# A routed-expert layer on one core: expert rows taken back to their tokens by TensorE and summed in SBUF, and the inputs of most experts fetched by indirect DMA

## The reference

```
x = x + concat(conv_out, pool_out) @ w_out
glog = hf @ w_rg + b_rg                    # hf = rmsnorm(x)
top_v, top_i = top_k(elog of the chosen group, 2)
w_top = softmax(top_v) * p_g
for e in range(32):
    a = silu(hf @ w_gate[e]) * (hf @ w_up[e])        # 2048 -> 512
    y = y + gates[:, e:e+1] * (a @ w_down[e])        # 512 -> 2048
x = x + y
y_prompt, y_sample = rmsnorm(x, g_final)
```

## Time and profile before

| what | value |
|---|---|
| median of 3 runs | 1323.94 us (1323.87 to 1324.67) |
| the profiled execution's own time | 1325.73 us |
| its span, first to last instruction | 1323.9 us |
| what lies around the span | 1.8 us |
| mean granted TensorE clock | 0.985 of full speed |
| TensorE busy, of the span | 94% |
| VectorE, ScalarE, GpSimd busy | 26%, 9%, 10% |
| HBM read, written | 457.20 MB, 20.80 MB |

### The profile page before, as it was taken

How to read it: one execution, slowest core, us unless ns; L and a number is a source line. 1 busy time by engine, 2 the same in 40 slices (tenths; PEclk the granted TensorE clock), 3 DMA queues, 4 the chain that set the end, 5 groups by cost and what they waited for, 6 DMA issues and landing times.

```text
span 1323.9 us, 15403 instructions
## 1 busy us (share of the span) xinstructions
PE 1240.6 (94%) x6286; PEld 686.6 (52%) x6286; DVE 350.8 (26%) x715; ACT 119.9 (9%) x242; POOL 134.1 (10%) x183
## 2 busy tenths in 40 slices
PE   9999999999999999988999999999999989989974
PEld 7777777777755445434443444434444544434421
DVE  5699974001342111120101011020101111010206
ACT  3100014000310000000000000000000000000022
POOL 6111394000000100000000000000000000000000
PEclk9999999999999999999999999999999999999998
DMA  9344424664579999999999999999999999999997
GB/s 289 136 151 149 142 96 147 248 254 159 210 281 416 409 429 426 427 430 430 427 430 431 430 430 425 429 429 428 430 429 433 428 430 427 428 428 427 424 422 264
DMA packets 77807, 465.26 MB, mean 351 GB/s; under 512 B 7263, under 2 KB 49375, under 8 KB 52243
## 3 DMA queue, kind: packets, MB, share of 16 engines
q1 hardware_dynamic: 71808, 455.36, 83.9%
q0 software_dynamic: 5392, 7.87, 2.0%
q10 hardware_dynamic: 571, 1.53, 0.3%
HBM read 457.20 MB, written 20.80 MB: 361 GB/s over the span
## 4 chain that ended last, share of the span: by engine, by line
PE 55%; DMA 42%; DVE 1%; ACT 0%; issue 0%; DVEq 0%; POOL 0%; SPq 0%; POOLq 0%
DMA arena<-in_w_up_dram 30%; PE bank L839 21%; PE bank L648 21%; DMA arena<-in_w_gate_dram 10%; PE bank L831 4%; PE bank L915 4%; DMA arena<-expert_rows 1%; PE bank L612 1%; PE bank L727 1%; DMA arena<-in_w_out_dram 1%; PE bank L596 1%; PE bank L745 0%; DVE arena L1464 0%; DVE arena L1476 0%; PE bank L581 0%
## 5 line engine op out<-in xcount | busy, mean ns | idle before, releaser
L839 PE MATMUL bank<-arena,xT 128*64 128x512 f32 x2040 | 456.5, 606 | 44.7 <-DMA arena<-in_w_up_dram 35.8
L839 PEld LDWEIGHTS bank<-arena,xT 128*64 128x64 f32 x2040 | 149.7, 140 | 348.9 <-issue 287.8
L648 PE MATMUL bank<-arena 128*128 128x288 f32 x1152 | 283.9, 408 | 0.0
L648 PEld LDWEIGHTS bank<-arena 128*128 128x128 f32 x1152 | 219.1, 191 | 63.5 <-issue 3.2
L915 PE MATMUL bank<-arena,aT 128*64 128x512 f32 x1024 | 228.7, 599 | 17.8 <-ACT aT L1129 15.2
L831 PEld LDWEIGHTS bank<-x1w,x1r 128*128 128x128 f32 x1536 | 173.9, 192 | 26.3 <-issue 25.2
L831 PE MATMUL bank<-x1w,x1r 128*128 128x128 f32 x1536 | 180.0, 277 | 0.9 <-ACT x1r L1094 0.9
L915 PEld LDWEIGHTS bank<-arena,aT 128*64 128x64 f32 x1024 | 72.5, 137 | 153.5 <-issue 138.7
L1495 DVE TENSOR_TENSOR a_sb<-sl_sb,bank 128x256 f32<-128x256 f32 x32 | 19.5, 608 | 476.0 <-ACT sl_sb L1127 476.0
L1658 POOL DMA_INDIRECT expert_rows<-ysb,cur_d x31 | 30.2, 973 | 836.7 <-DVE ysb L1515 809.9
L1240 DVE SCALAR_TENSOR_TENSOR arena<-arena,wdw 128x256 f32<-128x256 f32 x240 | 104.4, 514 | 0.1
(11 more groups left out here) (283 smaller groups left out, 446.5 us busy)
## 6 DMA issues: line engine op xcount, KB each, us to landing
arena<-in_w_down_dram SPq DMA_DIRECT2D x27, 4096.0 KB, 29.9
arena<-in_w_up_dram SPq DMA_DIRECT2D x41, 2048.0 KB, 20.7
arena<-in_w_gate_dram SPq DMA_DIRECT2D x19, 4096.0 KB, 26.7
arena<-in_w_gate_dram SPq DMA_DIRECT2D x16, 2048.0 KB, 20.5
arena<-in_w_up_dram SPq DMA_DIRECT2D x7, 4096.0 KB, 26.9
arena<-in_w_in_dram SPq DMA_DIRECT2D x11, 2048.0 KB, 8.1
arena<-in_w_gate_dram SPq DMA_DIRECT2D x19, 1024.0 KB, 9.7
arena<-in_w_out_dram SPq DMA_DIRECT2D x8, 2048.0 KB, 8.6
```

Source lines behind the costliest of these rows:

```text
L648: last = pe.matmul(ps[bank][:, 0:NTOK], wsl[a][:, k, cc * P:(cc + 1) * P], rhs[:, k, :], start=(n == 0), stop=(n == KT - 1))
L839: mm = pe.matmul(ps[4 + s][BLK * h:BLK * (h + 1), :], xgT[:, k, BLK * s:BLK * (s + 1)], w[:, :, 256 * h:256 * (h + 1)], start=(k == 0), st ...
```

## The change

The scatter of expert outputs, its DRAM tensor and the read back at the end are gone. In their place:

- `yrows` (the same SBUF as `ysb`) keeps a pair's 128 output rows whole, unscaled: two copies of 64 partitions by ScalarE and two by VectorE for each expert.
- For each pair VectorE makes `weighted_hot`, the one-hot table with the gate weights in it (six operations of 128x128, an add and a key update); TensorE transposes it in three pieces behind the second expert's gate and up, and VectorE copies the 288 columns to `to_token`.
- `combine_pair(i - 1)` runs behind gate and up of the first expert of pair i: four matmuls of 32 columns for the sample rows into bank 5 and eight of 128 columns by 512 for the prompt, into banks 2 and 3 in turn. VectorE adds each result to the token rows (`x1q`, and `acc_rows`, which lies in `x1r`), nine adds a pair. The third and later prompt matmuls wait for the add that frees their bank; down waits for all nine.
- ScalarE puts the residual rows in order in `acc_rows` during pair 0 (two copies of 128x2048, which stood before the last expert), and VectorE waits for them before pair 1.
- SyncE writes the 288 token rows to a DRAM tensor (2.36 MB) once the row copies are done, ahead of the first parts of expert 1. For pairs 2 to 15 GpSimd fetches 128 rows of 8 KiB by index, dropping empty slots, as soon as the fetch's buffer is free, which is when the inputs of the pair before are made.
- For those pairs `turn` takes the place of `select`: 16 matmuls in place of 48, with one scaled identity (`turn_table`) in place of `one_hot`.
- At the end all of pair 15 is combined on TensorE into eight banks, and added, squared and scaled in parts of 512 columns.
- The final gain's load waits for down of expert 30.

The core of the diff:

```diff
@@ sync, before the loop
             up_part(1, 1, 2, 8, ring_in[3])
+            sp.wait_ge(row_evac, 4 * TT)
+            for t in range(TT):
+                sp.dma_start(x1_dram[T0[t]:T0[t] + TS[t], :], x1r[0:TS[t], t, :]).then_inc(x1_out, 16)
             sp.wait_ge(row_mm, 4 * TT)
             load_first(1)
@@ tensor
+            def turn(m, b):
+                if b == 0:
+                    pe.wait_ge(rows_in, 16 * m - 16)
+                    pe.wait_ge(turn_ready, m - 1)
+                if b == 3:
+                    pe.wait_ge(xgT_ready, 4 * m + 1)
+                for k in range(4 * b, 4 * b + 4):
+                    last = pe.matmul(ps[SELB[b]][:, (k % 4) * P:(k % 4 + 1) * P], xrows[:, k * P:(k + 1) * P], turn_rows, start=True, stop=True)
+                last.then_inc(xgT_mm, 1)
+            def combine(t, c, bank):
+                return pe.matmul(ps[bank][:, :], to_token[:, T0[t]:T0[t] + P], yrows[:, c * QC:(c + 1) * QC], start=True, stop=True)
+            def combine_sample(bank):
+                for q in range(4):
+                    mm = pe.matmul(ps[bank][NS * q:NS * (q + 1), :], to_token[:, SEQ:NTOK], yrows[:, q * QC:(q + 1) * QC], start=True, stop=True)
+                return mm
+            def combine_pair(i):
+                pe.wait_ge(to_token_ready, i + 1)
+                pe.wait_ge(y0_ready, 2 * i + 2)
+                pe.wait_ge(y1_ready, 2 * i + 2)
+                combine_sample(5).then_inc(comb_mm, 1)
+                for n in range(8):
+                    if n >= 2:
+                        pe.wait_ge(comb_added, 9 * i + n)
+                    combine(n // 4, n % 4, 2 + n % 2).then_inc(comb_mm, 1)
@@ tensor, in pair()
+                    if s == 0 and not first:
+                        combine_pair(i - 1)
+                    if s == 1:
+                        pe.wait_ge(hot_w_ready, i + 1)
+                        for t in range(TT):
+                            ins = pe.transpose(ps[4][:, T0[t]:T0[t] + TS[t]], hot_w[0][0:TS[t], t, :], ident[0:TS[t], 0:TS[t]])
+                        ins.then_inc(to_token_mm, 1)
                     if ahead:
                         for b in ((0,), (1, 2, 3))[s] if first else (2 * s, 2 * s + 1):
-                            select(i + 1, b)
+                            if first:
+                                select(i + 1, b)
+                            else:
+                                turn(i + 1, b)
...
+                    if s == 0 and not first:
+                        pe.wait_ge(comb_added, 9 * i)
@@ vector
+            def add_combined(i):
+                dve.wait_ge(comb_mm, 9 * i + 1)
+                dve.tensor_tensor(x1q[:, :], x1q[:, :], ps[5][:, :], ALU.add).then_inc(comb_added, 1)
+                for n in range(8):
+                    dve.wait_ge(comb_mm, 9 * i + n + 2)
+                    part = acc_rows[n // 4][:, (n % 4) * QC:(n % 4 + 1) * QC]
+                    dve.tensor_tensor(part, part, ps[2 + n % 2][:, :], ALU.add).then_inc(comb_added, 1)
@@ gpsimd
-            def scatter_rows(rows, at, done):
-                pool.indirect_dma_start(out=yexp_dram, ...
+            def fetch_rows(i):
+                if isinstance(i, int) and i == 2:
+                    pool.wait_ge(x1_out, 16 * TT)
+                    pool.wait_ge(dst_ready, 4)
+                    pool.wait_ge(gu_used, 5)
+                else:
+                    pool.wait_ge(xgT_mm, 4 * i)
+                pool.tensor_copy(cur_t[:, :], dyn(tok_i, i, 1)).then_inc(cur_ready, 1)
+                pool.wait_ge(cur_ready, i - 1)
+                pool.sem_inc(waited, 1)
+                pool.indirect_dma_start(out=xrows, out_offset=None, in_=x1_dram,
+                                        in_offset=bass.IndirectOffsetOnAxis(ap=cur_t[:, 0:1], axis=0),
+                                        bounds_check=NTOK - 1, oob_is_err=False).then_inc(rows_in, 16)
```

More of the change, by code:

```diff
@@ L294, in hybrid_decoder_step @@
         old_out = sem("old_out")
-        y_out = [sem(f"y_out{s}") for s in range(2)]
+        x1_out = sem("x1_out")
+        rows_in = sem("rows_in")
         fin_out = sem("fin_out")
@@ L878, in pair @@
                     n, m = 2 * i + s, m0 + s
+                    if not first:
+                        if s == 0:
+                            pe.wait_ge(to_token_ready, i)
                     for c in range(4):
@@ L1146, in _ @@
             n_over = act.value_load(eid_i[0:1, 2 * OVP:2 * OVP + 1], min_val=0, max_val=2 * OVP)
-            pair(PAIRS - 1, last=True)
+            pair(PAIRS - 1)
             with act.If(n_over > 0):
@@ L1487, in last_one_hot @@
-                link(dve.memset(lastP, 0.0))
-            def pair(i, first=False, ahead=True, last=False):
+                    for t in range(TT):
+                        dve.tensor_scalar(hot_w[c][:, t, :], dealt[:, :], key[:, c, t:t + 1], wt[:, c, t:t + 1],
+                                          ALU.is_equal, ALU.mult).then_inc(hot_w_chain, 1)
+                dve.wait_ge(hot_w_chain, 7 * i + 6)
+                dve.tensor_tensor(hot_w[0], hot_w[0], hot_w[1], ALU.add).then_inc(hot_w_ready, 1)
@@ L1490, in pair @@
+            def pair(i, first=False, ahead=True):
                 for s in range(2):
                     n = 2 * i + s
-                    if last and s == 0:
-                        last_one_hot()
+                    if s == 0 and not first:
+                        if ahead:
+                            turn_table(i + 1)
+                        dve.wait_ge(hot_w_chain, 7 * i)
+                        weighted_hot(i)
                     dve.wait_ge(sl_ready, n + 1)
@@ L1549, in _ @@
             inverse_root(1, 1, 3)
-            dve.wait_ge(part_mm, 9)
-            dve.scalar_tensor_tensor(out=yq[:, 0, :], in0=ps[0][:, :], scalar=rs[:, 2:3], in1=gfq,
+            dve.scalar_tensor_tensor(out=fin_q, in0=x1q[:, :], scalar=rs[:, 2:3], in1=gfq,
                                      op0=ALU.mult, op1=ALU.mult).then_inc(out_ready, 1)
-            gain(1, 0, D // 2)
-            gain(1, D // 2, D)
+            for c in range(4):
+                gain(1, c)
         @block.gpsimd
@@ L1652, in _ @@
                 pool.wait_ge(s_ready, 2 * m + 2)
-            pool.wait_ge(yn_ready, 1)
-            pool.memset(ylast, 0.0).then_inc(zero_ready, 1)
-            def scatter_rows(rows, at, done):
-                pool.indirect_dma_start(out=yexp_dram, out_offset=bass.IndirectOffsetOnAxis(ap=at, axis=0),
-                                        in_=rows, in_offset=None, bounds_check=4 * NTOK - 1, oob_is_err=False).then_inc(done, 16)
-            def scatter(i, last=False, over=False):
-                for s in range(2):
-                    n = 2 * i + s
-                    if last and s == 1:
-                        pool.sem_inc(ysb_free[s], 1)
-                        pool.sem_inc(dcur_ready, 1)
-                        break
-                    if not (isinstance(i, int) and i == 0):
-                        pool.wait_ge(y_out[s], 16 * i - 16 * (s if over else 0))
-                    pool.sem_inc(ysb_free[s], 1)
-                    if isinstance(i, int) and i == 0:
-                        pool.wait_ge(dst_ready, 2)
-                    pool.tensor_copy(cur_d[:, s:s + 1], dyn(dst_i, n, 1)).then_inc(dcur_ready, 1)
-                    pool.wait_ge(dcur_ready, n + 1)
-                    pool.wait_ge(y0_ready, n + 1)
-                    pool.wait_ge(y1_ready, n + 1)
-                    pool.sem_inc(waited, 1)
-                    scatter_rows(ysb[:, s, :], cur_d[:, s:s + 1], y_out[s])
@@ L1688, in _ @@
+            fetch_rows(2)
+            with pool.Fori(3, PAIRS) as i:
+                fetch_rows(i)
             pool.wait_ge(over_ready, 1)
             n_over = pool.value_load(eid_i[0:1, 2 * OVP:2 * OVP + 1], min_val=0, max_val=2 * OVP)
[L1690 removed]
             with pool.If(n_over > 0):
                 with pool.Fori(0, OVP) as j:
[L1693 removed]
+                    fetch_rows(PAIRS + j)
 _INS = ["x_prompt", "x_sample", "state_conv", "state_pool", "g_mix", "w_in", "w_dw", "b_dw", "ln_g", "ln_b", "w_pool",
```

313 lines of the change are left out of this document (132 added, 181 removed).

## The result

The changed kernel takes **1328.77 us** (1325.38 to 1329.47, 8 runs) where the kernel before, run beside it, takes 1325.03 (1323.87 to 1327.9, 8 runs). The ratio is 1.0022, with an interval of 1.0013 to 1.0031: slower by 0.1 to 0.3%, about 3 us. The forecast was 1325.2, +1.3 on its own base. The profiled execution took 1329.0 us, its span (first to last instruction) is 1326.6, so 2.7 more than the span of before; around it lie 2.4 us, 0.6 more than before.

A forecast was written before the change was run, and what follows sets the result against it. Weights streaming by DMA were taken as the bound, with TensorE pacing up to 545 us. Terms +4.75, -0.7, +0.5, -0.6, -2.4 gave +1.5, by the times +1.3, which was taken: 1325.2 us, range 1318.5 to 1331.5.

The forecast's parts named there:

- The hole: SyncE's load at 456.9 us, behind down of expert 2, goes out 4.75 us later on an empty queue, delaying all weights.
- Combine is then 8.1 us: TensorE's combine of one pair: eight prompt matmuls at 0.90, 7.2 us, plus four sample matmuls side by side, 0.9.
- The three transposes cost 0.35: TensorE's transposes of the weighted table behind a pair's second gate and up: 0.35 us.
- Now about 1.0 us shows: In a pair's second expert, the last part of `turn` waits for its first part's eviction: about 1.0 us.
- No second hole: The next such load, at 483.96, moves only 2.4 us and meets a queue itself 4.75 late: no further loss.
- in the middle this costs nothing: Middle pairs: TensorE needs 56.2 of 59.3 us, so its added work costs 0 while weights are the bound.
- The last weights: Expert 31's releasing landing moves from 1276.1 to 1280.1; TensorE arrives at 1280.6, and last down ends at 1303.7.
- 4.75 - 0.7: Shift of expert 31's releasing landing: 4.75 us later by the early load, 0.7 earlier by fewer bytes moved.
- the end lies at D + 21.5: Stretch from the end of last down (D) to the end of the span: 21.5 us, was 23.9, so -2.4.
- Quarters one after another: Rival, slower: sample matmuls run serially, each combine 2.5 us longer, 1331; two at a time, 1327.2; 30% for both.
- Scatters cost more than their bytes: Rival, faster: removing scatters saves 0.5 us in each of 13 middle pairs, -7 us, 1318; chance 12%.
- Fetches late: Rival, slower: fetches landing at 30 us or more hold `turn`; at 35 us +28, 1353; chance 3%.

The follow-up runs named there:

- both mended: Changed kernel with combines of pairs 0 and 1 one expert later, three banks, sample product first, GpSimd's constant one operation shorter: 1321.74 us, 0.9973 of the kernel before.
- the holes alone: Changed kernel with only the combines of pairs 0 and 1 moved behind gate and up of experts 3 and 5, and three banks: 1321.67 us, 0.9977 of the kernel before.

## Why the prediction was right, and what it had wrong

The forecast of no clear change in either direction, by a hole early and a gain at the end, was right in its mechanism and too small by about 2 us. Most of the terms that were off were taken too small.

**The hole.** I expected the load of 456.91 at 461.7 after 4.75 us of lateness; it went at 462.82, 5.9 late, and 4 MiB landed after 12.6 us on an empty queue. "With an empty queue this is 4.75 us for the whole stream" holds: missing data in the window 4.9 us more than before, expert 28 later by 5.1, the run without pair 0's combine earlier by 6.8 there, apart from its start. The terms that were too small:

- "Combine is then 8.1 us": 1.00 + 7.63 = 8.63. The four sample quarters took 1.00, for 0.9 taken. The prompt products take 0.95 each in place of 0.90: a bank goes round in 1.91 us, where my sum had 1.79. The matmul (0.86) and the add (0.69 for 0.68) are as taken; the hops between the engines are 0.36, where I had 0.25. Three banks save the 0.57. Two adds of one combine, the second and the fourth of its nine (the first and third of the prompt, one bank):

```profile
617.20 0.69 DVE L1510 TENSOR_TENSOR x1r<-x1r,bank 128x512 f32<-128x512 f32 x1 [0.34 <-PE bank L836]
...
619.11 0.69 DVE L1510 TENSOR_TENSOR x1r<-x1r,bank 128x512 f32<-128x512 f32 x1 [0.36 <-PE bank L836]
```

- "The three transposes cost 0.35": 0.54.
- "Now about 1.0 us shows" (`turn`'s third part): in the trace TensorE is idle for 0.4, and the part behind it takes 0.3 more than it would in a row. This one errs the other way and came behind the hole, where it counted for nothing.
- The start, which had no term at all: expert 1 began at 400.3 against 399.8. Over the profiled executions of all versions it began at 397.1 to 400.8. GpSimd makes a small constant (`cdst`) whose two operations take 2.40 us in some executions and 0.47 or 0.48 in others, of whatever version, and the load that GpSimd issues behind it goes out some 2 us later (20.20 in the changed kernel, 18.07 when it ran again). But expert 1's start does not follow it: 397.7 to 400.8 in the five executions with 2.40, 397.1 to 399.8 in the seven with 0.47 or 0.48. What else scatters the start stays open. The scatter comes through to the end: expert 28 stands 793.6 to 794.1 us behind expert 1 in all six executions whose hole is the changed kernel's, with three banks or with two.

**No second hole.** Right for this kernel (442 GB/s at 518), and for the reason given, as the run with the combine moved shows by opening it.

**The middle.** TensorE needs 56.6 us a pair, predicted 56.2; the pairs take 59.35, predicted 59.3. All of "in the middle this costs nothing" stands. The group of `turn` from 601 to 1016 us, seven pairs, shows the stall that the slack hid:

```profile
L832 PE MATMUL bank<-x1w,xT 128*128 128x128 f32 x224 | 29.8, 281 | 2.6 <-DVE xT L1385 2.6
```

**The last weights.** The landing was forecast for 1280.1 and came at 1280.1. TensorE was to be there at 1280.6 and was at 1281.03. Last down was forecast to end at 1303.7 and ended at 1304.06. That the landing hit the forecast is in part luck: expert 28 was late by 5.1 where 4.75 - 0.7 was forecast, and the landing only by 4.1. From 1190 to 1300 us the indirect DMAs moved 0.07 MB where they had moved 0.40, which is 0.8 us at most; the rest of this 1.0 stays open.

**The end**, the term that failed most: "the end lies at D + 21.5", and it was D + 22.5. The copies were done 1.4 us behind down, as forecast, but the first product started only 2.46 us behind it, which the profile puts down to TensorE's own issue; of the last 1.0 us nothing that it waited for is seen. This is no fixed price. The gap is 1.59 us in the traces of seven other versions (pair 0 or pair 14 not combined, `turn` three times, the combine moved, three banks, both mended, the holes alone), whose stretch behind last down is 21.8 to 22.1 us, and 2.15 to 2.74 in the changed kernel and the others. No run shows what decides it. The gains cost 0.74 for 512 columns where half of a 1.24 (L1476) was 0.62. So -2.4 was -1.4. What lies around the span was taken as 1.8 us and was 2.4.

**The rivals.** *Quarters one after another* is wrong: 1.00 us for four. The page "TensorEngine Tiling (Array Packing)" of the Trainium skill, section Available Configurations, gives 128x32 four tiles, and here the trace agrees. A drain at the change of mode, as its Key Properties have it, costs little if anything: gate and up in front of the quarters takes 13.73 us as before, the quarters 0.10 more than the 0.9 estimated, and eight whole products behind them 7.13 (the run with the sample product first) where they take 7.03 with nothing of the kind in front. *Scatters cost more than their bytes* is wrong: the pairs take 59.35 us with one fetch and no scatter, as with two scatters, so 7 us were not to be had. *Fetches late* is wrong: 12.6 us at most, with 30 allowed.

The page "DMA: Bandwidth & Descriptors" of the Trainium skill, section Specifications, has besides the fabric's 435 GB/s a limit of about 358 GB/s for the HBM of one core, which its section Bandwidth gives for both cores of a pair streaming. Here one core streams alone: the slices of this kernel stand at 421 to 435 for 800 us, up to the first figure and far above the second; the measurement decides.

The chances put 0.39 on slower and 0.45 on no change; the result, 0.13 to 0.31%, lies across the line between them. What I should have done is to widen the forecast upwards: the quarters, the hops and the transposes were each taken at the low end of what their rows allow, and stood where each of them counts whole.

## What to carry to other kernels

Where loads fill the DMA engines without a pause, look at how long a load takes from issue to landing: where that is hardly more than its own size takes (13.4 us here, against 26.7 later), the queue is nearly empty, and whatever makes the next issue late is paid in full at the end, while the same work one expert later was free here. New work for TensorE should first go to where the queue is full; here the two moved combines with a third bank turned +0.26% into -0.23% on the same chip, 5.7 us of span. Two such holes are not added, the larger counts, so a mended one may show the next.

## What the runs showed of the hardware that was not expected

- Four matmuls of 32 columns by 512, float32, took 1.00 us together in four column quarters of the array; one of 128 columns took 0.86 (1308.46 - 1306.75 for two).
- The same two small operations on GpSimd (a constant of 128x3) take 0.48 or 2.40 us from one execution to another. The timeline's line of the changed kernel:

```profile
15.22 2.40 POOL L1619 TENSOR_SCALAR cdst<-tid_i 128x3 f32<-128x3 int32 x2
```

And that of the run without pair 14's combine:

```profile
14.91 0.48 POOL L1626 TENSOR_SCALAR cdst<-tid_i 128x3 f32<-128x3 int32 x2
```

- Some experts in the middle run their gate and up in 15.6 us in place of 13.95: 7 of the 22 from 566.09 to 1189.10 in the kernel before, 4 of the 21 from 601.16 to 1194.16 in the changed kernel. The granted clock is then 0.89 in the window. A wait of 2.2 to 2.7 us stands in front of each, but as long a wait does not always do it: in the kernel before, gate and up at 596.28 took 13.95 behind a wait of 2.92, and that of expert 31 took 13.95 behind 3.54, where the run without pair 14's combine took 15.65 behind 3.69. What decides stays open. One such from the timeline of the changed kernel:

```profile
660.74 15.59 PE L858 MATMUL bank<-arena,xT 128*64 128x512 f32 x64 [2.61 <-DMA arena<-in_w_up_dram]
```

The window over it:

```profile
660.00:676.00 16.00, 15.26 (x64) 4.79 (x64) 2.07 (x8) 0.00 (x0) 0.00 (x0) 0.89 1.02 436
```

Inside it the clock falls to 0.50, the lower of its two levels (1.2 GHz where full speed is 2.4), in the windows of 1 us from 661 to 664, and is at 0.96 from 664 to 665. It costs nothing there, since TensorE has 2.8 us to spare in a pair. In the changed kernel and its variants it costs its 1.7 us whole from expert 28 on, as in the profiled executions of the run with the combine moved and of that with the holes mended alone.
